# Experts in pairs: one shared block for the row tails of two experts in a hybrid encoder kernel

## The chip, the cores and the metric

The kernel runs on one core of a Trainium2 chip (trn2). The metric is the device time of one execution in microseconds (us), the median over several. A core has five engines, each with its own instruction stream: PE (TensorE, matmuls and transposes; its weight loads are shown as PEld), DVE (VectorE), ACT (ScalarE), POOL (GpSimd) and SP (SyncE, which here only starts DMAs). They meet at semaphores. The profile is one execution recorded by the hardware profiler.

## The reference

One encoder layer over two sequences (16 meta tokens with 256 prompt rows, 16 with 1024 sample rows, 1312 rows in all, 1024 wide, float32): a mixer (pooling and a bidirectional mLSTM), and then an expert-choice feed-forward. The change touches the second only:

```python
def expert_choice_ffn(h, w_router, w_gate, w_up, w_down):
    t = h.reshape(N, D)
    cap = CAPACITY_FACTOR * N // N_EXPERTS            # N_EXPERTS = 16, factor 2
    aff = softmax(t @ w_router)
    gate, idx = lax.top_k(aff.T, cap)                 # each expert chooses its rows
    xe = t[idx]
    hid = silu(xe @ w_gate[e]) * (xe @ w_up[e])       # 1024 x 1024 each
    ye = (hid @ w_down[e]) * gate[..., None]
    out = zeros(N, D).at[idx].add(ye)
```

Per expert this is 34 rows of the first sequence and 130 of the second, 164 together: one whole block of 128 rows and a tail of 36.

## The kernel before, in words

The first half of the program (lines up to about 1960) makes the mixer, the router and the ranking. The expert part follows. For each expert e:

- POOL gathers its 164 rows from DRAM into `xe`, block 0 of 128 rows and block 1 of 36 (`gather`, L790; the first expert at L785).
- PE transposes them, `transpose_rows` (L1961): 8 column tiles k, two blocks each, so 16 transposes of 128x128, four at a time into bank 6, and DVE copies each four out to `xeT` (`move_rows`, L1574). A transpose is a matmul against the identity, with the rows as the weights.
- PE runs `gate_up` (L1971) in four steps fp, each of 64 matmul records with 164 moving columns, ACT applies silu (L1218), DVE multiplies to `hidT` (`hidden`, L1580).
- PE runs `down` (L1992) in four steps of 32 records, ACT copies the results to `yeT` (L1227).
- PE transposes the results back, `transpose_results` (L2008), in four units m of four transposes: half of the columns by block (128 rows or 36). DVE scales each by the gate into `yeS` (`scaled`, L1584) and POOL adds the rows to the residual in DRAM by an indirect DMA (`scatter`, L801).

The order of work is written by hand. PE's stream (L2019 to L2051) is: the transposes of expert 0, its `gate_up`, then a hardware loop (`Fori`) of 14 passes: four times `transpose_rows(i + 1, m)` with `down(i, m)`, then four times `gate_up(i + 1, m)` with `transpose_results(i, m)`. So the transposes of the next rows stand between the steps of one expert's `down`, and those of the results between the steps of the next expert's `gate_up`. The last expert is written out behind the loop. The loops of ACT, DVE and POOL go along, one pass an expert; that of SP (L602) loads weights into a ring of six slots of 2 MB, each as soon as PE has left it. Waits count semaphores: `t_full`/`t_done` (rows transposed/copied), `hid_done`, `dn_full`/`dn_done`, `o_full`/`o_done` (results transposed/scaled), `acc_out` (scatters landed), `ye_free` (`yeS` may be written again), `xe_in` (gathers landed).

After the last but one expert the final RMSNorm of all rows is done beside the last expert, whose rows are finished apart.

Of the kernel before, what the change touches and what calls it, by code (L numbers as in the profile page):

```python
# [21 lines left out]
P = 128  # L22
# [127 lines left out]
def encoder_program(nc, x_prompt, x_sample, meta, g1, w_in, conv_w, conv_b, gate_b, pool_w, pool_scale,  # L150
# [10 lines left out]
    with ctx:  # L161
# [218 lines left out]
        xe = arena[:, 0:2 * D].rearrange("p (b n) -> p b n", b=2)  # L380
        BLKS = ((0, P), (1, SB_ROWS))

# [31 lines left out]
        xeT = arena[:, 2048:2048 + KT * SLOTS].rearrange("p (k s) -> p k s", k=KT)  # L414
        hidT = arena[:, 3360:3360 + KT * SLOTS].rearrange("p (k s) -> p k s", k=KT)
        sil = arena[:, 4672:4672 + 4 * SLOTS].rearrange("p (b f s) -> p b f s", b=2, f=2)
        yeT = arena[:, 5328:5328 + KT * SLOTS].rearrange("p (k s) -> p k s", k=KT)
        yeS = arena[:, 6640:6640 + 2 * D].rearrange("p (b n) -> p b n", b=2)
        cur_gather = sb("cur_gather", [P, 2, 1], U32)
        cur_scatter = sb("cur_scatter", [P, 2, 1], U32)  # L420
# [6 lines left out]
        passed, passed_pe = sem("passed"), sem("passed_pe")  # L427
# [4 lines left out]
        xl = arena[:, 8688:8688 + 2 * D].rearrange("p (b n) -> p b n", b=2)  # L432
# [8 lines left out]
        def gathered(e, m):  # L441

            return ps[FIRST_BANKS[m] if e is None else 6][:, :].rearrange("p (f s) -> p f s", f=2)
# [4 lines left out]
        with nc.Block() as block:  # L448

            @block.sync  # L450
            def _(sp):
# [158 lines left out]
                sp.wait_ge(acc_out, 32 * (NE - 1))  # L610
# [9 lines left out]
            def _(pool):  # L620
# [164 lines left out]
                for blk, n in BLKS:  # L785
                    pool.wait_ge(idx_ready, blk + 1)
                    pool.indirect_dma_start(out=xe[0:n, blk, :], out_offset=None, in_=t_d[:, :],
                                            in_offset=bass.IndirectOffsetOnAxis(ap=idxc[0:n, blk, 0:1], axis=0)).then_inc((xe_in, tail_in)[blk], 16)

                def gather(e, n_steps):  # L790

                    at = bass.ds(e, 1)
                    for blk, n in BLKS:
                        pool.tensor_copy(cur_gather[0:n, blk, :], idxc[0:n, blk, at]).then_inc(idx_step, 1)
                    pool.wait_ge(idx_step, n_steps + 2)
                    pool.sem_inc(passed, 1)
                    for blk, n in BLKS:
# [3 lines left out]
                def scatter(e, n_steps):  # L801

                    at = bass.ds(e, 1)
                    for blk, n in BLKS:
                        pool.tensor_copy(cur_scatter[0:n, blk, :], idxc[0:n, blk, at]).then_inc(idx_step, 1)
                    pool.wait_ge(idx_step, n_steps + 2)
                    pool.sem_inc(passed, 1)
                    pool.wait_ge(o_done, e * 4 + 5)
                    pool.sem_inc(passed, 1)
                    for blk, n in BLKS:  # L810
                        pool.indirect_dma_start(out=acc_d[:, :], out_offset=bass.IndirectOffsetOnAxis(ap=cur_scatter[0:n, blk, :], axis=0),  # L811
                                                in_=yeS[0:n, blk, :], in_offset=None, compute_op=ALU.add).then_inc(acc_out, 16)
                    pool.wait_ge(acc_out, e * 32 + 32)
                    pool.sem_inc(ye_free, 1)

                pool.sem_inc(ye_free, 1)
                pool.wait_ge(t_full, 4)
                gather(1, 0)
                with pool.Fori(0, NE - 2) as i:
                    pool.wait_ge(t_full, i * 4 + 8)  # L820
                    pool.sem_inc(passed, 1)
                    gather(i + 2, i * 4 + 2)
                    scatter(i, i * 4 + 4)
                pool.wait_ge(xe_in, 32 * NE - 16)
                scatter(NE - 2, 4 * NE - 6)
                pool.wait_ge(acc_out, 32 * (NE - 1))
                for blk, n in BLKS:
                    pool.tensor_copy(cur_scatter[0:n, blk, :], idxc[0:n, blk, NE - 1:NE]).then_inc(idx_step, 1)
                pool.wait_ge(idx_step, 4 * NE - 2)
# [11 lines left out]
            def _(act):  # L841
# [385 lines left out]
                def results_pair(e, dp):  # L1227
                    act.wait_ge(dn_full, e * 4 + dp + 1)
                    act.activation(yeT[:, 2 * dp:2 * dp + 2, :], pair_of_tiles(4 + dp % 2), ACT.Copy).then_inc(dn_done, 1)  # L1229

                def results(e):
                    for dp in range(4):
                        results_pair(e, dp)
# [12 lines left out]
                with act.Fori(0, NE - 2) as i:  # L1246
                    results(i)
                    silu(i + 1)
                results(NE - 2)
# [4 lines left out]
                for dp in range(4):  # L1254
                    results_pair(NE - 1, dp)
                    for i in FIN_AT[4 + dp]:
                        root_mean(i)
# [12 lines left out]
            def _(dve):  # L1270
# [243 lines left out]
                def take_ranked(blk):  # L1514
# [3 lines left out]
                    b = plan[("ix", blk)][0]  # L1518
                    st.do(dve.tensor_copy(idxc[0:n, blk, :], ps[b][0:n, 0:NE]))
# [3 lines left out]

                st.do(dve.memset(wr_wide, 0.0))
# [49 lines left out]
                def move_rows(e, first=False):  # L1574

                    for m in range(4):
                        dve.wait_ge(t_full, e * 4 + m + 1)
                        dve.tensor_copy(xeT[:, 2 * m:2 * m + 2, :], gathered(None if first else e, m)[:, :, 0:SLOTS]).then_inc(t_done, 1)  # L1578
# [5 lines left out]
                def scaled(e, m):  # L1584

                    h, (blk, n) = m // 2, BLKS[m % 2]
                    if m == 0:
                        dve.wait_ge(ye_free, e + 1)
                    dve.wait_ge(o_full, e * 4 + m + 1)
                    dve.tensor_scalar(yeS[0:n, blk, 512 * h:512 * h + 512], ps[7][0:n, :], gatec[0:n, blk, bass.ds(e, 1)], None,  # L1590
                                      ALU.mult).then_inc(o_done, 1)
# [8 lines left out]
                def last_rows(m):  # L1600
# [3 lines left out]
                    dve.wait_ge(o_full, (NE - 1) * 4 + m + 1)  # L1604
# [7 lines left out]
                move_rows(0, first=True)  # L1612
                for fp in range(4):
                    hidden(0, fp)
                with dve.Fori(0, NE - 2) as i:
                    move_rows(i + 1)
                    for m in range(4):
                        hidden(i + 1, m)
                        scaled(i, m)
                move_rows(NE - 1)  # L1620
                for m in range(4):
                    scaled(NE - 2, m)
# [22 lines left out]
            def _(pe):  # L1645
# [315 lines left out]
                def transpose_rows(e, m):  # L1961

                    pe.wait_ge(t_done, e * 4 + m)
                    to = gathered(e, m)
                    for a in range(2):
                        k = 2 * m + a
                        for blk in range(2):
                            last = pe.transpose(to[:, a, blk * P:(blk + 1) * P], xe[:, blk, k * P:(k + 1) * P], ident[:, :])  # L1968
                    last.then_inc(t_full, 1)

                def gate_up(e, fp, beside=None):  # L1971

                    if fp == 0:
                        pe.wait_ge(t_done, e * 4 + 3)
# [4 lines left out]
                    for w in range(2):  # L1979
                        for a in range(2):  # L1980
                            f = (2 * fp + a) % 4
                            for k in range(KT):
                                if fp + w + a == 0 and k == 6:
                                    pe.wait_ge(t_done, e * 4 + 4)
                                last = pe.matmul(ps[2 * w + fp % 2][:, a * SLOTS:(a + 1) * SLOTS], ring[2 * (fp // 2) + w][:, k, f * P:(f + 1) * P],  # L1985
                                                 xeT[:, k, :], start=k == 0, stop=k == KT - 1)
                            if w and a:
                                last.then_inc(gu_full, 1)
                            if beside is not None:
                                transpose_results(beside, 2 * w + a)  # L1990

                def down(e, dp):  # L1992
# [6 lines left out]
                    for a in range(2):  # L1999
                        dt = (2 * dp + a) % 4  # L2000
                        for k in range(KT):
                            if dp == 0 and a == 0 and k == 6:
                                pe.wait_ge(hid_done, e * 4 + 6)
                            last = pe.matmul(ps[4 + dp % 2][:, a * SLOTS:(a + 1) * SLOTS], ring[4 + dp // 2][:, k, dt * P:(dt + 1) * P],  # L2004
                                             hidT[:, k, :], start=k == 0, stop=k == KT - 1)
                    last.then_inc(dn_full, 1)

                def transpose_results(e, m):  # L2008

                    h, (blk, n) = m // 2, BLKS[m % 2]  # L2010
                    pe.wait_ge(dn_done, e * 4 + 2 * h + 4)
                    pe.wait_ge(o_done, e * 4 + m + 1)
                    if blk:
                        pe.sem_inc(passed_pe, 1)
                    for k in range(4):
                        last = pe.transpose(ps[7][0:n, k * P:(k + 1) * P], yeT[:, 4 * h + k, blk * P:blk * P + n], ident[:, :])  # L2016
                    last.then_inc(o_full, 1)

                for blk in range(2):  # L2019
                    pe.wait_ge((xe_in, tail_in)[blk], 16)  # L2020
                    for m in range(4):
                        to = gathered(None, m)
                        for a in range(2):
                            k = 2 * m + a
                            last = pe.transpose(to[:, a, blk * P:(blk + 1) * P], xe[:, blk, k * P:(k + 1) * P], ident[:, :])
# [12 lines left out]
                pe.wait_ge(xe_in, 32 * NE - 16)  # L2038
                for m in range(4):
                    transpose_rows(NE - 1, m)  # L2040
# [43 lines left out]
```

## Time and profile before

| what | value |
|---|---|
| median of 3 runs | 1795.99 us (1795.45 to 1797.01) |
| the profiled execution's own time | 1795.45 us |
| its span, first to last instruction | 1793.3 us |
| PE busy | 1749.6 us, 98% |
| DVE, ACT, POOL busy | 420.9, 387.9, 304.8 us |
| mean granted clock of TensorE | 0.992 of full speed |
| the loop of 14 passes | about 900.8 to 1697.9 us |
| mean DMA rate | 168 GB/s |

Busy time counts the time in which an engine executes; a PE that is always busy may still be slower than it could. A matmul record is some 0.3 us long but the next begins 0.14 us after it, so slots are read from starts and not from lengths. PEldq, SPq and the like are the engines' sequencers, which run ahead of the engines themselves.

### The profile page before, as it was taken

To read this page: it belongs to the slowest core of one execution; us is meant where nothing else is said; L and a number is where in the kernel's file an instruction comes from. 1 tells how busy PE (TensorE), PEld (TensorE's weight loads), DVE (VectorE), ACT (ScalarE), POOL (GpSimd) and SP (SyncE) were. 2 spreads that over 40 slices of the span, in tenths; PEclk is the share of its full clock that TensorE was granted. 3 is DMA by queue.
4 is the path that set the end of the run, shared out by engine and by line. 5 is a ranking of instruction groups with operands and counts; after the bars stand their busy time and mean duration, and the time that the engine had idled before them with its cause. 6 is when DMAs were issued, how large, how long until landed. Compare 5 with 4: busy or idle time off the path is not lost.

```text
span 1793.3 us, 25155 instructions
## 1 busy us (share of the span) xinstructions
PE 1749.6 (98%) x10427; PEld 1413.4 (79%) x10427; DVE 420.9 (23%) x909; ACT 387.9 (22%) x892; POOL 304.8 (17%) x344
## 2 busy tenths in 40 slices
PE   7999999999999999999999999999999999999996
PEld 4555556855555774455999999999999999999995
DVE  4471212621020560078110111011011110111114
ACT  3335224322131534464000000000000000000004
POOL 0071021520101244342001000110011100110010
PEclk9999999999999999999999999999999999999998
DMA  6110113421110535435568668686677767686685
GB/s 201 51 51 13 58 36 64 100 88 35 36 39 17 166 94 198 156 101 186 180 209 299 211 221 275 231 272 210 233 265 263 245 215 255 232 294 217 222 274 203
DMA packets 168828, 301.05 MB, mean 168 GB/s; under 512 B 11644, under 2 KB 53804, under 8 KB 168768
## 3 DMA queue, kind: packets, MB, share of 16 engines
q1 hardware_dynamic: 161904, 278.06, 45.5%
q0 software_dynamic: 6864, 22.17, 4.9%
q8 instruction: 40, 0.66, 0.2%
q14 instruction: 20, 0.16, 0.0%
HBM read 268.85 MB, written 31.35 MB: 167 GB/s over the span
## 4 chain that ended last, share of the span: by engine, by line
PE 96%; DVE 1%; ACT 1%; DMA 1%; issue 1%; POOL 0%; SPq 0%; DVEq 0%; POOLq 0%; ACTq 0%
PE bank L1985 32%; PE bank L2004 16%; PE bank L1763 12%; PE bank L1741 9%; PE bank L1894 8%; PE bank L1676 3%; PE bank L1711 2%; PE bank L1824 2%; PE bank L2016 2%; PE bank L1968 1%; PE bank L1805 1%; PE bank L1723 1%; PE bank L1719 1%; PE bank L1720 1%; PE bank L1843 1%; PE bank L1814 1%
## 5 line engine op out<-in xcount | busy, mean ns | idle before, releaser
L1985 PE MATMUL bank<-arena 128*128 128x164 f32 x4096 | 580.4, 303 | 0.8 <-DVE arena L1578 0.8
L1985 PEld LDWEIGHTS bank<-arena 128*128 128x128 f32 x4096 | 571.9, 190 | 1.2 <-DVE arena L1578 1.0
L2004 PE MATMUL bank<-arena 128*128 128x164 f32 x2048 | 295.3, 303 | 0.0
L2004 PEld LDWEIGHTS bank<-arena 128*128 128x128 f32 x2048 | 286.5, 190 | 0.0
L1763 PE MATMUL bank<-arena 128*128 128x512 f32 (+1 forms) x576 | 214.1, 534 | 0.0
L1763 PEld LDWEIGHTS bank<-arena 128*128 128x128 f32 x576 | 109.7, 191 | 102.8 <-issue 93.0
L1582 DVE TENSOR_TENSOR arena<-bank,arena 128x328 f32<-128x328 f32 x64 | 32.0, 499 | 583.9 <-ACT arena L1221 583.9
L1741 PE MATMUL bank<-arena 128*128 128x384 f32 x480 | 155.7, 485 | 0.0
L1221 ACT ACTIVATE arena<-bank 128x328 f32<-128x328 f32 x64 | 28.4, 443 | 562.8 <-PE bank L1985 562.8
L1894 PE MATMUL bank<-arena 128*128 128x512 f32 x320 | 146.4, 599 | 0.8 <-issue 0.8
L811 POOL DMA_INDIRECT residual<-arena,cur_scatter x30 | 46.0, 1534 | 581.9 <-DVE arena L1590 577.3
L1741 PEld LDWEIGHTS bank<-arena 128*128 128x128 f32 x480 | 90.8, 189 | 64.0
L1894 PEld LDWEIGHTS bank<-arena 128*128 128x128 f32 x320 | 57.5, 190 | 59.5 <-issue 59.4
L1384 DVE SCALAR_TENSOR_TENSOR arena<-arena,par 128x272 f32<-128x272 f32 (+1 forms) x48 | 41.9, 914 | 230.3 <-ACT arena L969 229.9
L1229 ACT ACTIVATE arena<-bank 128x328 f32<-128x328 f32 x64 | 28.3, 443 | 280.1 <-PE bank L2004 280.0
L1578 DVE COPY arena<-bank 128x328 f32<-128x328 f32 x64 | 31.4, 495 | 195.1 <-PE bank L1968 188.0
L1403 DVE SCALAR_TENSOR_TENSOR arena<-arena,spc,bank 128x193 f32<-128x193 f32 x120 | 42.8, 412 | 119.6 <-PE bank L1721 119.5
L1676 PE MATMUL bank<-arena 128*128 128x400 f32 x160 | 57.7, 513 | 0.4 <-DMA arena<-in_w_in 0.4
L699 POOL TENSOR_TENSOR arena<-arena 128x384 f32<-128x384 f32 x22 | 18.6, 864 | 192.1 <-ACT arena L1053 106.2
L847 ACT ACTIVATE arena<-bank 128x384 f32<-128x384 f32 (+1 forms) x47 | 24.0, 519 | 114.3 <-PE bank L1741 113.9
L1676 PEld LDWEIGHTS bank<-arena 128*128 128x128 f32 x160 | 30.5, 196 | 22.4 <-issue 2.7
L1590 DVE TENSOR_SCALAR arena<-bank,gatec 128x512 f32<-128x512 f32 (+1 forms) x60 | 44.3, 738 | 12.4 <-PE bank L2016 12.4
(244 smaller groups left out, 1512.1 us busy)
## 6 DMA issues: line engine op xcount, KB each, us to landing
arena<-in_w_up SPq DMA_DIRECT2D x32, 2048.0 KB, 12.8
arena<-in_w_down SPq DMA_DIRECT2D x32, 2048.0 KB, 10.4
arena<-in_w_gate SPq DMA_DIRECT2D x32, 2048.0 KB, 8.1
arena<-in_w_in SPq DMA_DIRECT2D x8, 1536.0 KB, 6.8
arena<-in_x_sample SPq DMA_DIRECT2D x14, 512.0 KB, 6.4
arena<-decay_rows SPq DMA_DIRECT2D x22, 256.0 KB, 4.9
arena<-state_rows SPq DMA_DIRECT2D x44, 128.0 KB, 4.2
residual<-arena SPq DMA_DIRECT2D x11, 512.0 KB, 6.7
```

Of the source, the lines that this page charges most:

```text
L811: pool.indirect_dma_start(out=acc_d[:, :], out_offset=bass.IndirectOffsetOnAxis(ap=cur_scatter[0:n, blk, :], axis=0), in_=yeS[0:n, blk, :] ...
L1384: st.do(dve.scalar_tensor_tensor(o, Z[:, lo + n_seq + n_tap:hi + n_seq + n_tap], par[:, c0:c0 + 1], o, ALU.mult, ALU.add))
L1403: last = dve.scalar_tensor_tensor(new[:, j, :], old[:, j, :], spc[:, a, i:i + 1], ps[b][:, c:c + VW], ALU.mult, ALU.add)
L1590: dve.tensor_scalar(yeS[0:n, blk, 512 * h:512 * h + 512], ps[7][0:n, :], gatec[0:n, blk, bass.ds(e, 1)], None, ALU.mult).then_inc(o_done, 1)
L1676: last = pe.matmul(ps[6 + i % 2][:, 0:OGW], hT[:, k, src], Wo[:, k, :], start=k == 0, stop=k == KT - 1)
L1711: last = pe.matmul(ps[b][:, 0:hi - lo], Wu[:, k, j * P:(j + 1) * P], hT[:, k, lo:hi], start=k == 0, stop=k == KT - 1)
L1741: last = pe.matmul(ps[b][:, 0:PAIR], hT[:, k, tile_cols(i)], Wb[nb % 2][:, k, :], start=k == 0, stop=k == KT - 1)
L1763: last = pe.matmul(ps[b][:, 0:hi - lo], Wb[nb % 2][:, k, j * P:(j + 1) * P], hT[:, k, lo:hi], start=k == 0, stop=k == KT - 1)
L1824: last = pe.matmul(set_[h][:, (1 - half) * VW:(2 - half) * VW], Pm[:, q * P:(q + 1) * P], v[:, i, h, :], start=False, stop=True, skip_grou ...
L1894: last = pe.matmul(ps[b][:, :], yT_t[n % 2][:, k * P:(k + 1) * P], wout[:, k, 512 * h:512 * h + 512], start=k == 0 and not whole, stop=k = ...
L1985: last = pe.matmul(ps[2 * w + fp % 2][:, a * SLOTS:(a + 1) * SLOTS], ring[2 * (fp // 2) + w][:, k, f * P:(f + 1) * P], xeT[:, k, :], start ...
L2004: last = pe.matmul(ps[4 + dp % 2][:, a * SLOTS:(a + 1) * SLOTS], ring[4 + dp // 2][:, k, dt * P:(dt + 1) * P], hidT[:, k, :], start=k == 0 ...
```

## The change

Experts 2j and 2j + 1 form a pair. Their 36-row tails share one block of 100 rows: the even tail in rows 0 to 35, the odd one in 64 to 99, with a gap of 28 between. A pair has three blocks: whole rows of the even expert, the tails, whole rows of the odd one. `xeT` and `yeT` hold 356 columns per k (`PAIR_W`), the even expert reads columns 0 to 163 and the odd one 192 to 355 (`SIDE`).

- Rows: 24 transposes a pair in place of 32, three per k into bank 6 and one DVE copy of 356 columns for them; eight such groups a pair, all among the steps of the odd expert's `down`, one at the start and one in the middle of each step.
- Results: 24 in place of 32 (six units u), units 0 and 1 (even expert, whole) behind the first two steps of the odd expert's `gate_up`, units 2 to 5 behind those of the next even expert. The last pair does its results by expert, as before.
- The hardware loops have 7 passes of a pair each in place of 14 of an expert. POOL gathers three blocks a pair (128, 100, 128 rows), and scatters four times a pair, waiting for each to land before the next.
- The first pair: the even whole and the tails first (two column tiles a bank, 228 columns each), and the odd expert's whole block, gathered once those are transposed, between the steps of expert 0's `gate_up`.
- DVE prepares index and gate columns for the tails' block (`idx_t`, `gate_t`) when the ranking is taken.

```diff
-        xe = arena[:, 0:2 * D].rearrange("p (b n) -> p b n", b=2)
+        xe = arena[:, 0:3 * D].rearrange("p (b n) -> p b n", b=3)
+        PAIRS = NE // 2
+        TAIL_AT = (0, 64)
+        TAILS = TAIL_AT[1] + SB_ROWS
+        PAIR_W = 2 * P + TAILS
+        SIDE = (0, PAIR_W - SLOTS)
+        WHOLE_AT, TAILS_AT = (0, P + TAILS), P
...
+                def scatter(j, n_steps):
...
+                    for col, (n, at, blk) in enumerate(((P, 0, 0), (P, 0, 2), (SB_ROWS, TAIL_AT[0], 1), (SB_ROWS, TAIL_AT[1], 1))):
+                        if col < 3:
+                            pool.wait_ge(o_done, j * 6 + 2 * col + 3)
+                            pool.sem_inc(passed, 1)
+                        add_rows(n, col, slice(at, at + n), blk)
+                        pool.wait_ge(acc_out, j * 64 + 16 * col + 16)
+                        pool.sem_inc(passed, 1)
+                    pool.sem_inc(ye_free, 1)
...
+                with pool.Fori(0, PAIRS - 1) as i:
+                    pool.wait_ge(t_full, i * 8 + 8)
+                    pool.sem_inc(passed, 1)
+                    gather(i + 1, i * 7)
+                    scatter(i, i * 7 + 3)
...
+                with dve.Fori(0, PAIRS - 1) as i:
                     for m in range(4):
-                        hidden(i + 1, m)
-                        scaled(i, m)
-                move_rows(NE - 1)
+                        hidden(i * 2 + 1, m)
+                        if m < 2:
+                            scaled_pair(i, m)
+                    for k in range(KT):
+                        move_rows(i + 1, k)
+                    for m in range(4):
+                        hidden(i * 2 + 2, m)
+                        scaled_pair(i, 2 + m)
...
-                def transpose_rows(e, m):
+                def transpose_rows(j, k):
 
-                    pe.wait_ge(t_done, e * 4 + m)
-                    to = gathered(e, m)
+                    pe.wait_ge(t_done, j * 8 + k)
+                    for blk, (at, n) in enumerate(((0, P), (TAILS_AT, TAILS), (WHOLE_AT[1], P))):
+                        last = pe.transpose(ps[6][:, at:at + n], xe[0:n, blk, k * P:(k + 1) * P], ident[0:n, 0:n])
+                    last.then_inc(t_full, 1)
...
+                def transpose_pair(j, u):
+
+                    h, at, n = u % 2, (0, WHOLE_AT[1], TAILS_AT)[u // 2], (P, P, TAILS)[u // 2]
+                    pe.wait_ge(dn_done, j * 8 + (0 if u < 2 else 4) + 2 * h + 4)
+                    pe.wait_ge(o_done, j * 6 + u + 1)
+                    for k in range(4):
+                        last = pe.transpose(ps[7][0:n, k * P:(k + 1) * P], yeT[:, 4 * h + k, at:at + n], ident[:, :])
+                    last.then_inc(o_full, 1)
...
                 for fp in range(4):
-                    gate_up(0, fp)
-                with pe.Fori(0, NE - 2) as i:
-                    pe.wait_ge(xe_in, i * 32 + 48)
+                    gate_up(0, None, fp, 4)
+                    if fp == 0:
+                        pe.wait_ge(xe_in, 32)
+                    transpose_first(4 + fp)
+                pe.wait_ge(gap_clear, 1)
+                with pe.Fori(0, PAIRS - 1) as i:
                     for m in range(4):
-                        transpose_rows(i + 1, m)
-                        down(i, m)
+                        down(i * 2, m)
                     for m in range(4):
-                        gate_up(i + 1, m)
-                        transpose_results(i, m)
+                        gate_up(i * 2 + 1, 1, m, i * 8 + 8)
+                        if m < 2:
+                            transpose_pair(i, m)
+                    pe.wait_ge(xe_in, i * 48 + 80)
+                    for m in range(4):
+                        transpose_rows(i + 1, 2 * m)
+                        down(i * 2 + 1, m, lambda: transpose_rows(i + 1, 2 * m + 1))
+                    for m in range(4):
+                        gate_up(i * 2 + 2, 0, m, i * 8 + 16)
+                        transpose_pair(i, 2 + m)
```

## Rows read from the trace of the kernel before

**Rows 1.** The page: the chain that ended last, by engine.
```profile
PE 96%; DVE 1%; ACT 1%; DMA 1%; issue 1%; POOL 0%; SPq 0%; DVEq 0%; POOLq 0%; ACTq 0%
```

**Rows 2.** Busy time (records) of PE, PEld, DVE, ACT, POOL; clock, DMA: one pass.
```profile
957.60:1014.60 57.00, 57.00 (x419) 56.84 (x418) 6.52 (x12) 3.58 (x9) 5.63 (x8) 1.00 0.72 244
```

**Rows 3.** Timeline, 957 to 964: start, length, engine, line, operation, count, idle before.
```profile
957.41 0.60 PE L2016 MATMUL bank<-ident,arena 128*36 128x128 f32 x4
957.75 0.37 SPq L607 DMA_DIRECT2D arena<-in_w_gate  x1
957.85 0.60 PE L1968 MATMUL bank<-ident,arena 128*128 128x128 f32 x4
958.09 0.50 DVE L1582 TENSOR_TENSOR arena<-bank,arena 128x328 f32<-128x328 f32 x1 [8.19 <-ACT arena L1221]
958.28 4.62 PE L2004 MATMUL bank<-arena 128*128 128x164 f32 x32
...
959.16 0.48 DVE L1578 COPY arena<-bank 128x328 f32<-128x328 f32 x1
960.08 1.65 POOL L811 DMA_INDIRECT residual<-arena,cur_scatter  x1 [40.03 <-DVE arena L1590]
...
962.74 0.60 PE L1968 MATMUL bank<-ident,arena 128*128 128x128 f32 x4
...
963.18 4.62 PE L2004 MATMUL bank<-arena 128*128 128x164 f32 x32
```

**Rows 4.** Groups by line and shape, whole span, the transposes: count, busy, mean ns.
```profile
L1968 PE MATMUL bank<-ident,arena 128*128 128x128 f32 x240 | 36.0, 273 | 0.0
L2016 PE MATMUL bank<-ident,arena 128*128 128x128 f32 x128 | 19.3, 273 | 0.5 <-ACT arena L1229 0.5
L2016 PE MATMUL bank<-ident,arena 128*36 128x128 f32 x128 | 19.2, 272 | 2.9 <-issue 2.9
```

**Rows 5.** DMA issues: count, KB each, median us to landing; last, line L811's own.
```profile
y_all<-arena SPq DMA_DIRECT2D x1, 128.0 KB, 2.4
...
arena<-state_rows SPq DMA_DIRECT2D x44, 64.0 KB, 3.6
...
arena<-ffn_in,cur_gather POOLq DMA_INDIRECT x30, 7.3
...
DMA to landing us min/median/max: 5.0/9.0/9.6
```

**Rows 6.** Timeline ahead of the loop, 857 to 901.
```profile
857.35 1.25 POOL L787 DMA_INDIRECT arena<-ffn_in,idxc  x1 [15.45 <-DVEq L1522]
...
862.45 1.97 PE L2025 MATMUL bank<-ident,arena 128*128 128x128 f32 x16 [1.37 <-DMA arena<-ffn_in,idxc]
863.80 1.72 DVE L1578 COPY arena<-bank 128x328 f32<-128x328 f32 x4 [7.03 <-PE bank L2025]
...
865.16 35.90 PE L1985 MATMUL bank<-arena 128*128 128x164 f32 x256 [0.75 <-DVE arena L1578]
```

**Rows 7.** PE's instruction fetches, MB: whole span, 865.2:900.7, 957.6:1697.9; and busy in 865.2:900.7.
```profile
q8 instruction: 40, 0.66, 0.2%
...
q8 instruction: 2, 0.03, 0.4%
...
q8 instruction: 1, 0.02, 0.0%
...
865.20:900.70 35.50, 35.50 (x255) 35.50 (x256) 1.82 (x4) 1.33 (x3) 1.88 (x2) 1.00 0.39 138
```

**Rows 8.** PE's fetches in 1695.9:1697.9; the loop's branch: min/median/max ns, first and last start.
```profile
q8 instruction: 1, 0.02, 3.0%
...
L2030 PEldq COMPARE_BRANCH  x14: 76/207/243, 955.6 to 1695.9; - x14
```

**Rows 9.** Busy time as in rows 2, two stretches in which PE waited (PEclk after POOL).
```profile
857.00:862.40 5.40, 4.08 (x23) 3.89 (x21) 0.00 (x0) 1.27 (x1) 2.15 (x2) 0.70 0.67 218
...
1768.00:1772.00 4.00, 2.09 (x17) 1.85 (x17) 3.17 (x5) 1.08 (x4) 0.00 (x0) 1.00 0.81 304
```

More of the change, by code:

```diff
@@ L439, in encoder_program, with gathered @@
         FIRST_BANKS = (6, 4, 5, 7)
[L441 to L443 removed]
+        def gathered(b, n, w):
+            return ps[b][:, 0:n * w].rearrange("p (f s) -> p f s", f=n)
         def pair_of_tiles(b):
@@ L784, in _ @@
                     pool.wait_ge(t_out[s], 16 * len(range(s, NT, 2)))
[L785 to L795, printed above, removed]
+                pool.wait_ge(idx_ready, 1)
@@ new lines, in _, with gather @@
+                pool.indirect_dma_start(out=xe[:, 2, :], out_offset=None, in_=t_d[:, :],
+                                        in_offset=bass.IndirectOffsetOnAxis(ap=idxc[:, 0, 1:2], axis=0)).then_inc(xe_in, 16)
+                def gather(j, n_steps):
+                    pool.tensor_copy(cur_gather[:, 0, :], idxc[:, 0, bass.ds(j * 2, 1)]).then_inc(idx_step, 1)
+                    pool.tensor_copy(cur_gather[0:TAILS, 1, :], idx_t[0:TAILS, bass.ds(j, 1)]).then_inc(idx_step, 1)
+                    pool.tensor_copy(cur_gather[:, 2, :], idxc[:, 0, bass.ds(j * 2 + 1, 1)]).then_inc(idx_step, 1)
+                    pool.wait_ge(idx_step, n_steps + 3)
@@ L796, in gather, with add_rows @@
                     pool.sem_inc(passed, 1)
-                    for blk, n in BLKS:
+                    for blk, n in ((0, P), (1, TAILS), (2, P)):
                         pool.indirect_dma_start(out=xe[0:n, blk, :], out_offset=None, in_=t_d[:, :],
                                                 in_offset=bass.IndirectOffsetOnAxis(ap=cur_gather[0:n, blk, :], axis=0)).then_inc(xe_in, 16)
-                def scatter(e, n_steps):
-                    at = bass.ds(e, 1)
+                def add_rows(n, col, rows, blk):
+                    pool.indirect_dma_start(out=acc_d[:, :], out_offset=bass.IndirectOffsetOnAxis(ap=cur_scatter[0:n, col, :], axis=0),
+                                            in_=yeS[rows, blk, :], in_offset=None, compute_op=ALU.add).then_inc(acc_out, 16)
@@ L804, in scatter @@
+                def scatter(j, n_steps):
                     for blk, n in BLKS:
-                        pool.tensor_copy(cur_scatter[0:n, blk, :], idxc[0:n, blk, at]).then_inc(idx_step, 1)
-                    pool.wait_ge(idx_step, n_steps + 2)
+                        for side in range(2):
+                            pool.tensor_copy(cur_scatter[0:n, 2 * blk + side, :], idxc[0:n, blk, bass.ds(j * 2 + side, 1)]).then_inc(idx_step, 1)
+                    pool.wait_ge(idx_step, n_steps + 4)
@@ L824, in _ @@
-                pool.wait_ge(xe_in, 32 * NE - 16)
-                scatter(NE - 2, 4 * NE - 6)
-                pool.wait_ge(acc_out, 32 * (NE - 1))
+                    gather(i + 1, i * 7)
+                    scatter(i, i * 7 + 3)
+                for blk, n in BLKS:
+                    pool.tensor_copy(cur_scatter[0:n, blk, :], idxc[0:n, blk, NE - 2:NE - 1]).then_inc(idx_step, 1)
+                pool.wait_ge(idx_step, 7 * PAIRS - 5)
+                pool.wait_ge(o_done, 6 * PAIRS - 1)
+                for blk, n in BLKS:
+                    add_rows(n, blk, slice(0, n), blk)
@@ L1245, in _ @@
                 silu(0)
[L1246 to L1249, printed above, removed]
+                with act.Fori(0, PAIRS - 1) as i:
+                    results(i * 2, 0)
+                    silu(i * 2 + 1)
+                    results(i * 2 + 1, 1)
+                    silu(i * 2 + 2)
+                results(NE - 2, 0)
                 for fp in range(4):
@@ L1518, in take_ranked @@
                     b = plan[("ix", blk)][0]
+                    if blk:
+                        even_odd = [ps[b][0:n, w * NE:(w + 1) * NE].rearrange("p (j s) -> p j s", s=2) for w in range(2)]
+                        for s in range(2):
+                            rows = slice(TAIL_AT[s], TAIL_AT[s] + n)
+                            st.do(dve.tensor_copy(idx_t[rows, :], even_odd[0][:, :, s]))
+                            st.do(dve.tensor_copy(gate_t[rows, :], even_odd[1][:, :, s]))
                     st.do(dve.tensor_copy(idxc[0:n, blk, :], ps[b][0:n, 0:NE]))
@@ L1572, in _, with move_first, move_rows @@
                 take_ranked(1)
[L1574 to L1578, printed above, removed]
+                def move_first(m):
+                    dve.wait_ge(t_full, m + 1)
+                    to, n, w = (xeT[:, 2 * m:2 * m + 2, 0:P + TAILS], FIRST_BANKS[m], P + TAILS) if m < 4 else (xeT[:, 2 * m - 8:2 * m - 6, P + TAILS:PAIR_W], 6, P)
+                    dve.tensor_copy(to, gathered(n, 2, w)).then_inc(t_done, 1)
+                def move_rows(j, k):
+                    dve.wait_ge(t_full, j * 8 + k + 1)
+                    dve.tensor_copy(xeT[:, k, :], ps[6][:, 0:PAIR_W]).then_inc(t_done, 1)
                 def hidden(e, fp):
@@ L1959, in _, with transpose_first, gate_up @@
                 keep_busy(14, ("af", 3))
-                def transpose_rows(e, m):
-                    pe.wait_ge(t_done, e * 4 + m)
-                    to = gathered(e, m)
+                def transpose_rows(j, k):
[3 more added lines that the diff above has]
+                    last.then_inc(t_full, 1)
+                def transpose_first(m):
+                    pe.wait_ge(t_done, m)
                     for a in range(2):
-                        k = 2 * m + a
-                        for blk in range(2):
-                            last = pe.transpose(to[:, a, blk * P:(blk + 1) * P], xe[:, blk, k * P:(k + 1) * P], ident[:, :])
+                        k = 2 * (m - 4) + a
+                        last = pe.transpose(gathered(6, 2, P)[:, a, :], xe[:, 2, k * P:(k + 1) * P], ident[:, :])
                     last.then_inc(t_full, 1)
-                def gate_up(e, fp, beside=None):
+                def gate_up(e, side, fp, rows_done, beside=None):
                     if fp == 0:
-                        pe.wait_ge(t_done, e * 4 + 3)
+                        pe.wait_ge(t_done, rows_done - 1)
                     if fp % 2 == 0:
@@ L1983, in gate_up, with down @@
                                 if fp + w + a == 0 and k == 6:
-                                    pe.wait_ge(t_done, e * 4 + 4)
+                                    pe.wait_ge(t_done, rows_done)
                                 last = pe.matmul(ps[2 * w + fp % 2][:, a * SLOTS:(a + 1) * SLOTS], ring[2 * (fp // 2) + w][:, k, f * P:(f + 1) * P],
-                                                 xeT[:, k, :], start=k == 0, stop=k == KT - 1)
+                                                 xeT[:, k, SIDE[side or 0]:SIDE[side or 0] + SLOTS], start=k == 0, stop=k == KT - 1)
                             if w and a:
                                 last.then_inc(gu_full, 1)
-                            if beside is not None:
-                                transpose_results(beside, 2 * w + a)
-                def down(e, dp):
+                            if beside:
+                                transpose_results(NE - 2, 0, 2 * w + a, 6 * PAIRS - 5 + 2 * w + a)
+                def down(e, dp, between=None):
                     if dp % 2 == 0:
@@ L2005, in down, with transpose_results @@
                                              hidT[:, k, :], start=k == 0, stop=k == KT - 1)
+                        if a == 0 and between is not None:
+                            between()
                     last.then_inc(dn_full, 1)
-                def transpose_results(e, m):
+                def transpose_results(e, side, m, before):
                     h, (blk, n) = m // 2, BLKS[m % 2]
+                    at = ((0, P), (SIDE[1] + SB_ROWS, SIDE[1]))[side][blk]
                     pe.wait_ge(dn_done, e * 4 + 2 * h + 4)
-                    pe.wait_ge(o_done, e * 4 + m + 1)
-                    if blk:
-                        pe.sem_inc(passed_pe, 1)
+                    pe.wait_ge(o_done, before)
                     for k in range(4):
-                        last = pe.transpose(ps[7][0:n, k * P:(k + 1) * P], yeT[:, 4 * h + k, blk * P:blk * P + n], ident[:, :])
+                        last = pe.transpose(ps[7][0:n, k * P:(k + 1) * P], yeT[:, 4 * h + k, at:at + n], ident[:, :])
                     last.then_inc(o_full, 1)
-                for blk in range(2):
+                def transpose_pair(j, u):
[3 more added lines that the diff above has]
+                    for k in range(4):
+                        last = pe.transpose(ps[7][0:n, k * P:(k + 1) * P], yeT[:, 4 * h + k, at:at + n], ident[:, :])
+                    last.then_inc(o_full, 1)
+                for blk, (at, n) in enumerate(((0, P), (TAILS_AT, TAILS))):
                     pe.wait_ge((xe_in, tail_in)[blk], 16)
                     for m in range(4):
-                        to = gathered(None, m)
+                        to = gathered(FIRST_BANKS[m], 2, P + TAILS)
                         for a in range(2):
                             k = 2 * m + a
-                            last = pe.transpose(to[:, a, blk * P:(blk + 1) * P], xe[:, blk, k * P:(k + 1) * P], ident[:, :])
+                            last = pe.transpose(to[:, a, at:at + n], xe[0:n, blk, k * P:(k + 1) * P], ident[0:n, 0:n])
                         if blk:
```

94 lines of the change are left out of this document (49 added, 45 removed).

## Prediction

> **What bounds the kernel now.** I read the chain of waits first, then busy time by stretch, then the timeline of one expert. PE (TensorE) holds 96% of the chain that ended last [rows 1]. In the expert loop it is never idle: one pass of 57 us has 57.00 us of PE busy, and DVE, ACT and POOL about 6.5, 3.6 and 5.6 us [rows 2]. The reader is to see that an instruction taken from PE's stream there shortens the span by its whole slot, that nothing taken from another engine does, and that a new stop in PE's stream costs in full.
>
> **The slot of a transpose.** In a `down` step [rows 3] 32 matmul records of 164 columns start at 958.28, four transposes at 962.74 and the next records at 963.18. So four transposes take 0.44 us, 0.110 each, and a matmul record takes 4.46/32 = 0.139. The transposes of 36 rows (128\*36) at 957.41 are followed by the next four at 957.85, again 0.44: a tail costs as much as a whole block. That is what the change attacks.
>
> **Transposes removed.** Rows in: 240 + 16 = 256 now [rows 4, 6]; afterwards 8 pairs x 8 x 3 = 192, so 64 fewer. Results: 2 x 128 = 256 now; afterwards 7 pairs x 24, and the last pair keeps its 32, which is 200, so 56 fewer. 120 x 0.110 = **13.2 us off PE**. The 64 remaining tail transposes of rows in stream 100 identity columns in place of 128. No row has that width; from the two slots above, (139 - 110)/36 = 0.8 ns a column, hence 23 ns each, 1.5 us; bounds are 0 (something else sets the slot) and 1.5. I take 1.5, since the slots of 128 and 164 columns lie on one line through nearly zero. The results' tails still stream 128 columns: nothing.
>
> **Covers that get thinner, none gone.** After the last gate/up step of an expert, ACT and DVE must finish `hidden`: ready at 958.09 + 0.50 = 958.59, 1.2 us after PE leaves gate/up at 957.41 [rows 3]. PE needs it at its 13th `down` record. Now 8 transposes and 12 records, 2.5 us, cover it; afterwards 4 + 12 (2.1 us) on even experts, 3 + 12 (2.0) on odd ones, 2 + 12 (1.9) on expert 0. No wait; if I am wrong by the whole margin it is some 0.5 us times 15. Rows in use only bank 6: three transposes, DVE's copy (356 columns by 0.48/328, 0.53 us, behind `hidden`, so done 1.7 us after gate/up), and the next three come after 16 records, at 2.6 us. Covered. Fewer, larger DVE copies: hidden either way.
>
> **POOL.** Four scatters a pair now go one after another, the two tails last, and DVE's first scaling of the next pair waits for them. Counted from the pair's last transposes (957.41 in the rows): POOL issues at +2.7; two in series at 9.0 us each [rows 5] end near +21. In the loop that is wanted after four `down` steps and one gate/up step, +0.4 + 17.8 + 8.9 = +27. Covered. The last pair wants it earlier: PE's next transposes come two quarters into the first gate/up step, so the rows must be free by about +22.4. Margin 1 us, none at 9.6 us a scatter; bounds 0 and +3, I take 0. POOL's third gather, for expert 1, starts at about 864.6 and needs 7.3 us [rows 5], to 872; PE wants it after one gate/up step, 865.2 + 8.9 = 874. Covered. The weight loads on SP keep their waits and order; they have spare time, PE never waits for one.
>
> **Before the loop** everything is exposed, since PE waits for the gathers and for DVE's copies [rows 6]. The four copies take 1.72 us for 328 columns each; at 456 columns the three that gate/up waits for are 0.5 us longer. The tail gather fetches 100 rows in place of 36 (bounds 0 and +1.2 us; I take +0.4), and four more small DVE copies ahead of it end before POOL has issued the first gather (858.6). Together **+0.9**. The end, after expert 14, keeps its steps: 0.
>
> So the work alone gives -13.2 - 1.5 + 0.9 = **-13.8 us**.
>
> **The loop body, doubled.** PE's code comes in by its own DMA queue: 40 fetches, 0.66 MB, so 16 KB each [rows 7]. In 865.2 to 900.7 PE takes 255 matmuls and 256 weight loads and there are 2 fetches: 256 instructions a fetch. The body now has 416 matmul and 416 weight-load records [rows 2] and by my count of the code 22 waits, register steps and a branch: 854, or 3.3 blocks. In its 13 repeats from 957.6 to 1697.9 there is a single fetch, and that falls into 1695.9 to 1697.9, just after the last branch [rows 7, 8]. Two things follow. Four blocks and the one fetched ahead, five, are kept over a branch back. And the body ends just short of a block's end, so it starts 4.0 - 3.3 = 0.6 to 0.7 into a block. The new body has 816 matmuls, 816 weight loads and about 54 others, 1686 or 6.6 blocks, and starts some 20 instructions later: it ends 7.3 blocks after the start of its first one. It touches 8 blocks, and with the one ahead 9 must be kept for the first to be there when the branch goes back, 6 times. The rows show 5 kept and nothing of 9. If the first block is gone, PE's sequencer stops at every branch back until it is fetched.
>
> Price of one: the sequencer takes the first branch from 955.6 to 955.8 [rows 8], while PE starts the transposes behind it at 957.85 [rows 3]; it is some 2.1 us ahead, and that much is covered. The fetch itself has no row from request to landing. The shortest load in the trace lands after 2.4 us, 64 KB loads after 3.6, gathers beside the weights after 7.3 [rows 5]. Exposed: 0.3, 1.5 or 5.2 us. I take 3.6 (small, hardware queue), so 1.5, times 6 = **+9.0**; bounds +1.8 and +31. The gap might also bring TensorE's lower clock: over 857.0 to 862.4, with PE busy for 4.08 of 5.4 us, the mean granted clock was 0.70, so part of it at the 1.2 GHz level and 0.30 x 5.4 = 1.6 us of clock lost; but it stayed 1.00 over 1768 to 1772 with 2.09 of 4 us busy [rows 9]. Bounds 0 and +10 (six times 1.6), taken 0.
>
> The Trainium skill has a rule for this (Runtime: NRT & Kernel Launch, Instruction fetch mechanics): PE's instruction memory is 128 KiB, a FIFO refilled in 16 KiB blocks, and a taken branch to a block outside it waits for a DMA. By that, 8 blocks are kept where 9 are wanted. The same section also speaks of a window of two pages; the trace disagrees with that for PE, since four blocks went round without a fetch. No run here shows the 128 KiB yet; by that rule case B below would be out.
>
> **Sum.** The profiled execution took 1795.45 us (span 1793.3 and 2.15 around it), the lowest of three with median 1795.99. 1795.45 - 13.8 + 9.0 = **1790.7**.
>
> **Cases.**
> A, the forecast: first block refetched at each of 6 branches, exposed 0.5 to 2.3 us each: 1784.6 to 1795.5, centre 1790.7. For it: 9 blocks against 5 shown. Against it: nothing shows the size of the store. Chance 0.40.
> B: the store holds the whole body. No fetch in the repeats, 1795.45 - 13.8 = 1781.7, 1780.5 to 1783. For it: the old loop never refetched. Chance 0.35.
> C, the other side: the refetch lands late. It is requested just as PE finishes gate/up, where SP starts two 2 MB weight loads (957.75 in [rows 3]), as the gathers that need 7.3 us also run beside weights. Exposed 5.2 us, 31 us in all: 1813. It makes the kernel slower than before once a branch exposes more than 13.8/6 = 2.3 us, a fetch of 4.4 us; a spell at the low clock at each branch does the same with a 3.6 us fetch (1801). Chance 0.20.
> D: a cover above or the last scatter chain fails by a few us without any refetch, 1783 to 1788. Chance 0.05.
>
> A measurement of this kernel tells about 0.2%, 3.6 us, from no change. B and D are faster by that; A is for fetches under about 3.8 us, some 0.45 of its chance, and otherwise within it; of C nearly all is slower. Faster 0.35 + 0.05 + 0.18 = 0.58, same 0.22 + 0.02 = 0.24, slower 0.18. The range goes from B's lower end, 1780, to 1803, into C; what is left out is most of C and a little below. A's own range is 1784 to 1796.
>
> **What would show it.** L1968's and L2016's successors with 120 transposes fewer, at 0.44 us for four and 0.33 for three. Instruction fetches of PE: about 2 to 9 in every repeat (A, C), or none (B), and PE idle at six places about 112 us apart, right ahead of a `down` of an even expert, put down to "issue". Two experts without that gap last 114.0 - 1.9 = 112 us. I am wrong if fetches occur in every repeat and PE has no gap, if gaps come elsewhere (DVE copy, `hidden`, o_done), or if PE's busy time in the loop does not fall by the 13 us.

## The result, and the profile after

The changed kernel takes 1799.87 us (median of 19 runs, 1797.67 to 1802.80), the kernel before 1796.47 beside it: a ratio of 1.0018, interval 1.0011 to 1.0025. It is slower by 0.2% (3.4 us between the medians, 3.2 by the ratio), a small difference but clear of the noise, where 1790.7 and "faster" had been forecast. The work went from PE as counted, and two stops at each of six branches took it back and a little more. The profiled execution took 1797.67 us with a span of 1795.9.

The page of the changed kernel: PE's busy time, the fetches of PE's code, and the groups of `down` (L2062), whose last number is the idle time ahead of them.

```profile
PE 1737.0 (97%) x10307; PEld 1400.8 (78%) x10307; DVE 414.8 (23%) x902; ACT 388.4 (22%) x892; POOL 296.1 (16%) x327
...
q8 instruction: 97, 1.59, 0.4%
...
L2062 PEld LDWEIGHTS bank<-arena 128*128 128x128 f32 x2048 | 286.7, 190 | 15.4 <-issue 15.4
```

PE has 12.6 us less to do than its 1749.6 before, and 120 matmul records fewer (10307 for 10427). But its weight loads, idle for nothing in this group before, now wait 15.4 us for "issue", that is, for the instruction itself. And the 40 fetches of [rows 7] have become 97. The idle time ahead of this group, 15.4 us, is what the two stops cost at all six branches together.

Busy time of PE, PEld, DVE, ACT and POOL, clock and DMA, in one pass of the loop, from branch to branch; it answers to two passes of [rows 2]:

```profile
1128.60:1243.30 114.70, 112.55 (x818) 112.04 (x817) 12.08 (x22) 7.09 (x16) 9.99 (x14) 1.00 0.71 245
```

Two passes were 113.9 us (by the branch's starts in [rows 8]); one is 114.7 now and holds 2.7 us in which PE loads no weights.

The timeline at the second of these branches: start, length, what, and in brackets the idle time ahead of it with its cause.

```profile
1128.42 0.60 PE L2084 MATMUL bank<-ident,arena 128*100 128x128 f32 x4
...
1129.10 0.50 DVE L1620 TENSOR_TENSOR arena<-bank,arena 128x328 f32<-128x328 f32 x1 [8.19 <-ACT arena L1244]
...
1130.49 4.75 PEld L2062 LDWEIGHTS bank<-arena 128*128 128x128 f32 x34 [1.72 <-issue]
1130.49 5.00 PE L2062 MATMUL bank<-arena 128*128 128x164 f32 x34 [1.47 <-DVE arena L1620]
...
1136.16 0.99 PEld L2062 LDWEIGHTS bank<-arena 128*128 128x128 f32 x7 [0.92 <-issue]
```

Each row merges consecutive operations of one kind, so x34 is 34 weight loads or matmuls. This is how such a stop reads, and how it misleads. The matmul row blames DVE (`hidden`), but DVE was done at 1129.60 and PE started 0.9 us later; the weight load on the row above says "issue", and the experiments below bear it out. The second stop comes after exactly 34 pairs of weight load and matmul, at this branch and at the other five.

The loop's branch on PE's sequencer (count; shortest, median, longest in ns; first and last start), and the fetches of code between two branches (1126.6 to 1241.2), against one in 740 us of [rows 7]:

```profile
L2102 PEldq COMPARE_BRANCH  x7: 76/3441/3861, 1012.1 to 1699.8; - x7
...
q8 instruction: 9, 0.15, 0.5%
```

The branch that goes back took 0.21 us [rows 8] and takes 3.44 us now. Nine fetches are one for each of the 8 blocks the body touches and one more, for the block behind the body: it is fetched ahead, shortly before the branch, and not used.

The transposes, in the timeline of the same kernel: three transposes, and the 16 records that begin 0.31 us later.

```profile
1185.85 0.47 PE L2018 MATMUL bank<-ident,arena 128*128 128x128 f32 x3
1186.16 2.39 PE L2062 MATMUL bank<-arena 128*128 128x164 f32 x16
```

Three take 0.31 us where 0.33 would be three of [rows 3]: the narrower tail costs about 0.09.

### The profile page after: what moved, and what is told of

Read it like the earlier page. It is cut to its first block, busy times and chain, and to the rows that moved or that the text cites. A ratio compares the mean times of both kernels' runs of the same rounds, so it can differ in the third digit from the quotient of the medians.

```text
span 1795.9 us, 24895 instructions
## 1 busy us (share of the span) xinstructions
PE 1737.0 (97%) x10307; PEld 1400.8 (78%) x10307; DVE 414.8 (23%) x902; ACT 388.4 (22%) x892; POOL 296.1 (16%) x327
## 4 chain that ended last, share of the span: by engine, by line
PE 94%; ACT 2%; DVE 2%; issue 1%; DMA 1%; POOL 0%; SPq 0%; DVEq 0%; POOLq 0%; ACTq 0%
PE bank L2043 32%; PE bank L2062 15%; PE bank L1816 12%; PE bank L1794 9%; PE bank L1947 8%; PE bank L1729 3%; PE bank L1764 2%; PE bank L1877 2%; PE bank L1858 1%; PE bank L1776 1%; PE bank L1773 1%; PE bank L1772 1%; PE bank L2018 1%; PE bank L1896 1%; PE bank L2084 1%
## 5 line engine op out<-in xcount | busy, mean ns | idle before, releaser
L2062 PE MATMUL bank<-arena 128*128 128x164 f32 x2048 | 298.0, 303 | 12.5 <-DVE arena L1620 7.0
L2062 PEld LDWEIGHTS bank<-arena 128*128 128x128 f32 x2048 | 286.7, 190 | 15.4 <-issue 15.4
L1616 DVE COPY arena<-bank 128x356 f32<-128x356 f32 x56 | 29.5, 527 | 94.4 <-PE bank L2018 94.4
L931 ACT ACTIVATE arena<-bank 128x240 f32<-128x240 f32 (+2 forms) x42 | 19.2, 457 | 112.6 <-PE bank L1816 98.0
```

## The experiments

Two theories stood against each other. R: the doubled body no longer fits PE's instruction store, and each branch back waits for a fetch. H: the thinner cover of `hidden` lets PE wait for ACT and DVE, as the matmul row says. Each time below is a median, with its lowest and highest, and the ratio is to the kernel before, with its 95% interval.

**The loop written out.** PE gets the same instructions without a branch.

```diff
-                with pe.Fori(0, PAIRS - 1) as i:
+                for i in range(PAIRS - 1):
```

> The changed kernel with PE's loop of 7 passes written out, so that PE has no branch; all other engines keep their loops. Theory R (instruction refetch: each of the 6 branches back finds its block and the next one gone from PE's instruction store): the stops of some 1.7 and 1.0 us behind each branch go, 6 x 2.55 = 15.3 us, so 1799.9 - 15.3 = 1784.5 us, and PE's fetches of code come one at a time, every 256 instructions, at no cost. Rival H (the stops are waits for the hidden activations, whose cover the change made thinner): nothing of it depends on the branch, 1799.9 us, and gaps stay ahead of down of every even expert.

Measured: 1784.86 us (1784.35 to 1787.49), ratio 0.9943 (0.9930 to 0.9957). The stops are gone: PE is busy for 112.00 us of the 112 us from 1117 to 1229. H falls, since the program still waits for `hidden` with the same cover. Its DVE row starts 0.68 us behind the last transposes of the pass in both kernels (1128.42 and 1129.10 above, 1128.47 and 1129.15 here), and here `down` starts at 1128.91, 0.44 us behind the same transposes, without a stop. The fetches are 82, one for every 256 instructions, and none is seen to hold PE up:

```profile
q8 instruction: 82, 1.34, 0.3%
```

**The loop kept, its code moved by 120 instructions.** Increments of a semaphore that nobody waits for go among the matmuls of expert 0 (the matmul's own line is shortened here).

```diff
                                 last = pe.matmul(...)
+                                if side is None and fp * 32 + w * 16 + a * 8 + k < 120:
+                                    pe.sem_inc(passed_pe, 1)
```

> The changed kernel, loop kept, with 120 semaphore increments that nobody waits for put between the matmuls of expert 0's gate and up products, so the loop body lies 120 instructions later. 
Measured: 1785.25 us (1784.42 to 1786.83), ratio 0.9942 (0.9928 to 0.9956). Nothing in the loop changed except where its code lies. The fetches of the whole span, the branch, and one pass of this kernel:

```profile
q8 instruction: 43, 0.70, 0.2%
...
L2104 PEldq COMPARE_BRANCH  x7: 76/208/235, 1012.7 to 1684.7; - x7
...
1012.70:1124.70 112.00, 112.00 (x818) 111.98 (x817) 12.09 (x22) 7.09 (x16) 9.95 (x14) 1.00 0.74 250
```

112.00 us a pass, all of it PE's, as the prediction had for a pair without stops. The branch is back at 0.21 us.

**Moved by 50.** The same edit with 50.

> The same with 50 increments: the body starts 231 instructions into a block, 25 ahead of the next one, and still touches 8 blocks. Theory R: the first stop stays (1.7 us), and the second comes after some 25 instructions, when PE has 1.8 us of work or less in its queue, so it is exposed for 3.5 - 1.8 = 1.7 to 2.3 us in place of 1.0: 6 x 0.7 to 1.3 longer than the changed kernel, 1804 to 1808 us. If padding itself helps or harms in another way, this and the run with 120 go the same way. Rival H: 1799.9.

Measured: 1832.52 us (1829.83 to 1833.85), ratio 1.0202 (1.0188 to 1.0216). The direction is the one that R gave and H did not have: padding by 50 costs and by 120 gains. The size was wrong: 32.7 us over the changed kernel where I gave 4 to 8, because I took the second block to be there when the branch ends. The timeline of PE's weight loads behind the first branch (1015.5), then the group's idle time over the whole run, and the busy times and clock (the number after POOL's) around the second stop:

```profile
1019.38 1.41 PEld L2064 LDWEIGHTS bank<-arena 128*128 128x128 f32 x10 [1.74 <-issue]
1024.64 4.50 PEld L2064 LDWEIGHTS bank<-arena 128*128 128x128 f32 x21 [3.84 <-issue]
...
L2064 PEld LDWEIGHTS bank<-arena 128*128 128x128 f32 x2048 | 297.6, 196 | 36.0 <-issue 36.0
...
1017.50:1024.70 7.20, 2.11 (x15) 1.62 (x13) 1.16 (x2) 0.44 (x1) 1.41 (x1) 0.98 0.79 289
1024.70:1030.00 5.30, 5.30 (x27) 5.30 (x28) 0.00 (x0) 0.43 (x1) 1.38 (x1) 0.70 1.05 372
```

The second stop is 3.84 us, after 10 pairs. With PE busy for only 2.11 of 7.2 us, the granted clock then falls: 0.70 over the next 5.3 us, part of it at the 1.2 GHz level, which is 0.30 x 5.3 = 1.6 us lost. The twelve stops, the second ones of 3.8 to 4.7 us, add up to 36.0 us. The other 11 of the 47 us over the run with 120 fit a spell at the lower clock behind each of the six second stops, of which this one cost 1.6 us.

**The old kernel with two experts a pass.** No pairing, the same work, half as many branches.

```diff
-                with pe.Fori(0, NE - 2) as i:
-                    pe.wait_ge(xe_in, i * 32 + 48)
+                with pe.Fori(0, NE // 2 - 1) as j:
+                    for i in (j * 2, j * 2 + 1):
+                        pe.wait_ge(xe_in, i * 32 + 48)
...
```

> The kernel before, with nothing of the pairing, but PE's loop has 7 passes of two experts in place of 14 of one. The work is the same to the last transpose. Theory R: the body of some 1700 instructions touches 8 blocks, so 6 branches with a stop of 1.7 and one of about 1.0 us: 1796.5 + 15 = 1811 to 1812 us. Rival H, or any other that sees the cost in the pairing: 1796.5 us, no change.

Measured: 1808.17 us (1807.01 to 1810.46), ratio 1.0070 (1.0056 to 1.0084). The doubled body alone makes the kernel 11.7 us slower, with nothing of the pairing in it. Less than the 15 expected, because the second stop is shorter here, or missing: this body begins earlier in its block and runs 41 pairs ahead of it. On the weight loads the six first stops add up to 10.5 us, and the second ones are 0.4, 1.2 and 0.4 us at three branches and none at the other three. Timeline of PE and the branch:

```profile
1130.03 0.65 PE L1968 MATMUL bank<-ident,arena 128*128 128x128 f32 x4 [1.44 <-issue]
...
1135.90 1.38 PE L2004 MATMUL bank<-arena 128*128 128x164 f32 x8 [0.18 <-issue]
...
L2030 PEldq COMPARE_BRANCH  x7: 83/3609/3787, 1010.5 to 1706.6; - x7
```

**The old kernel with its loop written out.** As the first edit, on `with pe.Fori(0, NE - 2) as i`.

> The kernel before with PE's loop of 14 passes written out. Theory R: its loop of 854 instructions never refetched, so there is nothing to gain: 1796.5 us, within 1. The pairing's own worth is then this time less that of the changed kernel written out (1784.9), 11.6 us. Rival: a branch back costs PE something even where its block is kept (0.2 us of the sequencer by its row, covered by the 2 us that it is ahead); written out, the kernel before gains up to 13 x 0.2 = 2.7 us.

Measured: 1796.85 us (1793.76 to 1798.98), ratio 1.0003 (0.9994 to 1.0012). No change within the interval: 13 branches whose block is kept cost PE nothing that shows. So the pairing itself is worth 1796.85 - 1784.86 = 12.0 us.

**Moved by 176 and by 200: where does the store end?** The edit as above, with one increment after each of the 128 matmuls of expert 0's gate and up products and a second after the first 48 or 72.

> The changed kernel, loop kept, 176 increments ahead of it. The body starts at 101 of 256 and its 1681 instructions end at 1782, inside the 7th block (1792). A store of 8 blocks: 7 and the one ahead fit, no fetch in the repeats, 1785 us, as with 120. If the store kept fewer or the padding of 120 worked otherwise (for example by moving single instructions): between 1785 and 1800.

> The same with 200 increments, 24 more. The body starts at 125 and ends at 1806, 14 instructions into an 8th block: with the one ahead 9 blocks, so the first is gone again at each of the 6 branches. First stop 1.6 to 1.9 us; the second does not come: the second block is there some 9.3 us after the branch in the three runs that had stops, and PE now has 131 instructions, some 65 pairs or 9 us, in the first block behind a stop of 3.7 us from the branch. 1785.3 + 6 x 1.65 = 1795 us. Rival (the size of the store has nothing to do with it, 176 and 200 are alike): 1785.

Measured: 1785.31 us (1783.21 to 1787.20), ratio 0.9944 (0.9930 to 0.9957), and 1796.39 us (1795.01 to 1800.40), ratio 1.0003 (0.9994 to 1.0012). Twenty-four more increments ahead of the loop cost 11.1 us. Six stops of 1.6 to 1.9 us, 10.2 us in all on the weight loads, are most of it. Branch and fetches of the one with 176:

```profile
L2105 PEldq COMPARE_BRANCH  x7: 76/208/240, 1013.6 to 1685.6; - x7
...
q8 instruction: 44, 0.72, 0.2%
```

and of the one with 200, with the stop, which is now the only one of its pass:

```profile
L2105 PEldq COMPARE_BRANCH  x7: 76/3438/3688, 1015.4 to 1697.7; - x7
...
q8 instruction: 98, 1.61, 0.4%
...
1133.19 0.99 PEld L2065 LDWEIGHTS bank<-arena 128*128 128x128 f32 x7 [1.68 <-issue]
```

By the count, the body ends 10 instructions ahead of the end of a 7th block in the one and 14 into an 8th in the other. A body that touches 8 blocks is fetched whole in every pass, 9 fetches with the one ahead, and a body that touches 7 is never fetched again. So the store keeps 8 blocks of 256 instructions, the one fetched ahead among them. The Trainium skill gives the same size (Runtime: NRT & Kernel Launch, Instruction fetch mechanics: 128 KiB for PE, in blocks of 16 KiB), and the two runs agree with it. The "only 2 cache lines" of the same section of the Trainium skill do not hold for PE: 7 blocks go round here without a fetch.

## Why the prediction was wrong, point by point

The mechanism of case A came true, and its size was off: the term "exposed 1.5, times 6 = +9.0" measured 15.4 us, 10.2 in the first stops and 5.2 in second ones that the prediction did not have. That is 2.6 us a branch, more than the 2.3 at which the prediction itself put the turn from faster to slower. From the forecast to the result it goes 1790.7 + 6.4 (the stops) + 1.8 (a gain of 12.0 and not 13.8) + 1.0 (the sum started from 1795.45, and the median of 19 is 1796.47) = 1799.9. The result lies within the stated range, 1780 to 1803, but that is luck: A's own range ended at 1795.5, and the part above it was there for case C, whose story did not happen.

- **The refetch at each branch: right.** Nine blocks were wanted and 8 are kept. The body is 1681 instructions by the count of records between two branches (1686 forecast), starts 0.71 into a block (181 of 256, since 34 pairs and some 7 other instructions run ahead of the second stop) and ends 7.27 after that block's start (7.3 forecast).
- **The price of one fetch: right.** The branch stops the sequencer for 3.44 us (3.6 taken), its lead of 2 us covers its part, and 1.5 to 2.0 us shows on the weight loads (1.5 taken), 10.2 us for six.
- **The step that failed: one fetch a branch.** The prediction counted the first block alone: "if the first block is gone". The second was gone as well, and it did not come at once. In the fetch records of all four kernels that refetch, the first block's fetch starts 0.9 to 1.5 us behind the branch's start, and the second's 6.9 to 7.4 us behind it (once 8.3), whatever is left of the first block; why so late, no run here shows. Where PE stops for it, its code runs 9.2 to 9.8 us behind the branch (10.7 at the late fetch): 1015.46 to 1024.64 with 50, 1126.59 to 1136.16 in the changed kernel, 1126.16 to 1135.90 with two bodies. PE has by then only the queue and the rest of the first block to work on. That rest was 34 pairs, 4.7 us, in the changed kernel: a second stop of 0.7 to 1.0 us, 5.2 us in all. With 10 pairs it is 3.8 to 4.7 us, with 41 at most 1.2 and nothing at three of six branches, with some 65 (200 increments) never. One number, how far from a block's end the loop begins, orders all four. The prediction had it ("0.6 to 0.7 into a block") and used it only to count blocks.
- **The late-fetch case (C): wrong as told.** The branch takes 3.3 to 3.9 us in every kernel that refetches (medians 3.4 to 3.6), not 7.3, though the weight loads start beside it. What can make a branch cost more than C's 5.2 us is the second block and the clock: in the run with 50 a pass was 7.9 us longer than with 120.
- **The clock: right to leave out, for this kernel.** It stayed at 1.00 in all passes of the changed kernel; stops of 1.7 and 1.0 us did not lower it, and in the run with 50 it fell behind stops of 1.7 and 3.8.
- **The work: near.** 120 transposes fewer at 0.110 us, a pass of 112.00 us in place of 113.9, tails of 0.09 us: as counted. The whole gain is 12.0 us (loops written out on both sides) for 13.8 forecast. The start cost what was taken, within what two pairs of traces can tell: from the ranking's transposes to the first gate/up matmul the kernel before has 855.79 to 865.16, 9.4 us, the changed one 854.84 to 865.79, 10.95, so +1.6; with the loops written out it is 854.07 to 864.84 and 854.64 to 866.06, so +0.65; +0.9 was taken. The rest is clock, for which the prediction has no term here. With the loops written out, gate/up of expert 0 takes 37.05 us before and 38.84 changed, at a mean granted clock of 0.97 and 0.94; with the loops kept it was 36.17 and 36.61, at 1.00. So spells at the 1.2 GHz level cost 0.9 and 2.2 us, 1.3 more in the changed kernel. From the first `down` on the changed kernel is 15.16 us shorter, and 0.44 of that (36.61 - 36.17) is work moved ahead of it: 14.7, where 13.2 + 1.5 was counted. Whether the change has a part in the longer spell is not shown: with the loops kept, neither kernel has one in this stretch.
- **The covers and the scatters: right.** With the stops removed PE has no idle time in a pass at all, so no wait for `hidden`, for DVE's copies or for `ye_free` costs PE anything. POOL has the last scatter landed (1718.6) before the first scaling of the last pair wants its rows (1722.8): 4.2 us of margin, where the prediction had 1.

## What to carry to other kernels

A hardware loop on PE has a size, and the size is measured in blocks touched, not in instructions: count the loop's records, find where its code starts in a block, and keep the body at 7 blocks or fewer, since the eighth of the store holds what is fetched ahead. A body that must be longer is better entered far from the end of its first block, since what is left of that block covers the wait for the second. If a restructuring makes a body longer, write the loop out, or move it: here both turned a change that lost 0.2% into one that gains 0.6%. In a profile, read a gap in the matmuls on the weight-load row, and look at the fetches of code and at the branch's own duration before you believe the engine that is named.

## What the runs showed of the hardware

- PE's code comes in blocks of 256 instructions (16 KB), and 8 of them are kept; straight code of 82 blocks is fetched with no cost that shows (1784.86 us written out, 1785.25 with a loop that fits).
- A branch to a block that is gone takes 3.4 to 3.6 us instead of 0.21, of which about 2 are covered by what PE has queued. The block behind it is there 9.2 to 9.8 us after the branch (once 10.7), since its fetch starts some 6 us after the first one's. I had expected it with the first one.
- The fastest version here is the changed kernel with PE's loop written out or its code moved by 120 or 176: 1784.9 to 1785.3 us, 0.6% under the kernel before.
- Open: why the second fetch starts so late. Not tried: whether the store can be filled in another way than in order, and the same sizes on another engine.
